# Merging stage, norm, router and the first context projections as ordered lists

## The reference, cut to what matters

```python
merged = merged + gates[:, :, n] * (o_n @ w_branch[l, n])          # four branches
x = layer_norm(DEEPNORM_ALPHA * x + merged @ w_out[l], ln1_g[l], ln1_b[l])
y = hierarchical_moe(x, r_group, r_group_b, r_expert, r_expert_b, e_gate, e_up, e_down)
x = layer_norm(DEEPNORM_ALPHA * x + y, ln2_g[l], ln2_b[l])
```

```python
h_c = modulate(rms_norm(x_ctx, g_attn[l]), csh1, csc1)      # 256 x 1024
p = h_c @ w_in                                              # c_q 768, c_kv 256, k_r 32, na 3 x 512, gates
mq = rms_norm(c_q, g_qa) @ w_uq ;  kv = rms_norm(c_kv, g_kva) @ w_ukv
# then attention over the context, its merge, its output product and its MLP
```

## Time and profile before

| | us |
|---|---|
| median of three runs | 4213.06 |
| the profiled execution's own time | 4211.14 |
| its span in the profile | 4209.2 |
| last product of the merge begins | 1024.00 |
| first product of the output stage begins | 1034.22 |
| first expert product begins | 1182.35 |
| sections 0 to 2 stand on TensorE | 1207.4 to 1251.4 |
| section 6's product | 1365.91 to 1379.9 |

### The profile page before, as it was taken

How to read it: one execution, slowest core, us unless ns; L and a number is a source line. 1 busy time by engine, 2 the same in 40 slices (tenths; PEclk the granted TensorE clock), 3 DMA queues, 4 the chain that set the end, 5 groups by cost and what they waited for, 6 DMA issues and landing times. The chain is left out here.

```text
span 4209.2 us, 38458 instructions
## 1 busy us (share of the span) xinstructions
PE 3767.7 (90%) x14796; PEld 2139.7 (51%) x14796; DVE 1752.0 (42%) x3047; ACT 757.3 (18%) x1690; POOL 169.3 (4%) x377
## 2 busy tenths in 40 slices
PE   7987777799578999999967899999998899999999
PEld 3653663444334344555533545458744455447844
DVE  0128643344413211111134655355446556445545
ACT  0212201111012211100113434110001354211000
POOL 1001000000010000000020300000000300000000
PEclk9989777799689999999988999999999999999999
DMA  7443001223157768888753111132222201122221
GB/s 297 174 159 112 1 5 50 95 95 130 72 203 295 282 240 326 350 343 344 305 201 109 61 41 40 70 110 80 80 80 86 103 21 61 58 83 80 80 80 60
DMA packets 197192, 574.67 MB, mean 137 GB/s; under 512 B 24324, under 2 KB 34356, under 8 KB 183752
## 3 DMA queue, kind: packets, MB, share of 16 engines
q1 hardware_dynamic: 177704, 518.35, 32.8%
q10 hardware_dynamic: 11424, 27.37, 1.9%
q0 software_dynamic: 7888, 26.53, 1.8%
HBM read 540.49 MB, written 31.73 MB: 136 GB/s over the span
## 5 line engine op out<-in xcount | busy, mean ns | idle before, releaser
L342 PE MATMUL ps<-out_sums 128*128 128x256 f32 (+1 forms) x1152 | 333.6, 450 | 2.3 <-issue 2.3
L342 PE MATMUL ps<-mixers_xT,ring 128*128 128x512 f32 (+2 forms) x928 | 306.9, 491 | 1.6 <-PEq L272 0.9
L342 PEld LDWEIGHTS ps<-out_sums 128*128 128x128 f32 x1152 | 218.7, 190 | 114.2 <-issue 94.5
L342 PEld LDWEIGHTS ps<-mixers_xT,ring 128*128 128x128 f32 (+1 forms) x928 | 173.5, 188 | 130.3 <-issue 115.2
L342 PE MATMUL ps<-ring,mixers_xT 128*128 128x512 f32 (+2 forms) x608 | 219.3, 517 | 9.9 <-DVE ab_qk L336 6.0
L342 PE MATMUL ps<-ring,layers_hT 128*128 128x512 f32 x416 | 186.7, 606 | 18.7 <-PEq L272 16.9
L2205 PE MATMUL ps<-ring,moe_xgT 128*64 128x512 f32 x432 | 191.8, 601 | 3.2 <-issue 2.3
L342 PEld LDWEIGHTS ps<-ring,mixers_xT 128*128 128x128 f32 x608 | 117.0, 205 | 108.6 <-issue 94.1
L342 PE MATMUL ps<-ring,out_hidden 128*128 128x512 f32 x384 | 167.4, 592 | 0.0
L2206 PE MATMUL ps<-ring,moe_xgT 128*64 128x512 f32 x368 | 163.1, 599 | 0.0
L342 PEld LDWEIGHTS ps<-ring,layers_hT 128*128 128x128 f32 x416 | 79.6, 194 | 120.0 <-issue 116.0
(11 more groups left out here) (895 smaller groups left out, 6170.1 us busy)
## 6 DMA issues: line engine op xcount, KB each, us to landing
ring<-in_w_ff SPq DMA_DIRECT2D x45, 2048.0 KB
ring<-in_w_in SPq DMA_DIRECT2D x40, 2048.0 KB
ring<-in_e_down SPq DMA_DIRECT2D x27, 2048.0 KB
ring<-in_e_gate SPq DMA_DIRECT2D x25, 2048.0 KB
ring<-in_e_up SPq DMA_DIRECT2D x25, 2048.0 KB
ring<-in_w_ada SPq DMA_DIRECT2D x24, 2048.0 KB
ring<-in_w_out SPq DMA_DIRECT2D x8, 2048.0 KB
deep_ring_more<-in_e_gate SPq DMA_DIRECT2D x8, 2048.0 KB, 7.8
```

What stands on the lines that cost most here:

```text
L342: last = pe.matmul(out, lhsT, rhs, start=(j == 0), stop=(j == len(pairs) - 1))
```

## The change

The merge's output stage becomes a single list. It begins with the transposes of half the merged rows, then the first four groups of the output product, the other transposes, the sums of rows. The norm is worked row tile by row tile inside the list; rows 0 and 1 are normed while the last products run. The seven products come in another order (the sixth pair, `out[5]`, ahead of `out[4]`). Between them stand the context's norm and its transposes (`work`, `turned`), and after them c_kv and k_r (`kv`, `kr`). The normed rows are stored by ScalarE, tile by tile.

The router becomes a list too, with the same steps, and c_q's four groups stand in it: one between the logits and the ranks, three behind the ranks. Section 6's product of near queries (`head`) stands ahead of the transposes of the first experts' rows. The weight tiles of sections 0, 1, 2 and 6 move forward accordingly. What is left of sections 0 and 2 (their norms) stays after pair 0's down product.

Some buffers move: the context's transposed rows have their own, its rows and the low-rank results lie in the branches' outputs, the experts' transposed rows in the first block's `xT`. The context rows are loaded twice: for the norm at the output stage's start, and again in the experts' block for the later residual, which waits for them (`x_landed`).

`CTX_COSTS` changes, and with it the places. Sections 3 to 5 now stand after pair 0, 6 (its norm) and 7 after pair 1, 8 after pair 2, 9 to 11 after pair 3, 12 to 14 after pair 4, none after pair 5, 15 and 16 after pair 6, 17 and 18 after 7, 19 and 20 after 8, 21 alone after 9, then two a pair after pairs 10 to 14, and 32 alone after pair 15.

```diff
+        flat = M.mixed[:, :, :, :].rearrange("p i k n -> p (i k n)")
+        self.low = flat[:, 0:TC * D].rearrange("p (t d) -> p t d", d=D)
+        self.x = flat[:, TC * D:].rearrange("p (t d) -> p t d", d=D)
+        self.q, self.ckv = self.low[:, :, 0:Q_LORA], self.low[:, :, Q_LORA:D]
+        self.hT = st.sb("c_hT", [P, DK, CTX])
+        self.k_r = st.sb("c_k_r", [P, TC, ROPE])
...
+        M.early = t0 + 2
 
         def load(sp):
-            sp.dma_start(x[:, :, :], by_rows(A["x"][0])).then_inc(st.sig["x"], 16)
+            for t in range(TC):
+                sp.dma_start(C.x[:, t, :], A["ctx_2"][0][t * P:(t + 1) * P, :]).then_inc(sig[f"c_x{t}"], 16)
+            sp.dma_start(x[:, :, :], by_rows(A["x"][0])).then_inc(sig["x"], 16)
...
-        made = row_sums(a, S)
-        gs, _, _ = seven(M, t0, t0 + 1, a, S, made, R, [parts[:, x_, 4, :] for x_ in range(2)],
-                         lambda x_, i, j: parts[:, x_, 2 * i + j, :], done)
-        products(M, "wout_p", made + sum(gs, []), tiles=2, extra={"sync": load})
-        layer_norm(M, "ln1", x, TT, A["ln1_g"][0], A["ln1_b"][0])
-        def save(sp):
-            sp.dma_start(by_rows(M.x1), x[:, :, :]).then_inc(st.sig["saved"], 16)
-            sp.wait_ge(st.sig["saved"], 16)
-        products(M, "x1T", transposes(M, lambda t, j: x[:, t, j * P:(j + 1) * P],
-                                      lambda j, a, n: M.xT[:, j, a * P:(a + n) * P], TT, DK),
-                 extra={"sync": save})
+        top, rest = (half_transposes(M, merged, M.xT, r) for r in range(2))
+        made = row_sums(a, S, tuple(top + rest))
+        out, ends, _ = seven(M, t0, t0 + 1, a, S, made, R, [parts[:, x_, 4, :] for x_ in range(2)],
+                             lambda x_, i, j: parts[:, x_, 2 * i + j, :], done)
+        for b in out[0]:
+            if b.pe:
+                b.needs += tuple(top)
+        def statistics(dve, link, t):
+            link.post(dve.bn_stats(stats[:, t, 0, :], x[:, t, 0:BANK]))
+            link(dve.bn_stats(stats[:, t, 1, :], x[:, t, BANK:D]))
+            return dve.bn_aggr(mv[:, t, :], stats[:, t, :, :])
+        def normalise(dve, link, t):
+            if t == 0:
+                dve.wait_ge(sig["gains"], 32)
+            link(dve.reciprocal(rs[:, t:t + 1], rs[:, t:t + 1]))
+            link(dve.tensor_scalar(x[:, t, :], x[:, t, :], mv[:, t, 0:1], rs[:, t:t + 1], ALU.subtract, ALU.mult))
+            link(dve.tensor_tensor(x[:, t, :], x[:, t, :], g[:, 0, :], ALU.mult))
+            return dve.tensor_tensor(x[:, t, :], x[:, t, :], g[:, 1, :], ALU.add)
+        counted = [group(None, lambda dve, _, link, t=t: statistics(dve, link, t), "v", after=(ends[t, 0], ends[t, 1]))
+                   for t in range(TT)]
+        roots = [group(None, lambda act, _, link, t=t: act.activation(
+            rs[:, t:t + 1], mv[:, t, 1:2], ACT.Sqrt, bias=M.ln_eps[:, :]), "s", after=(counted[t],)) for t in range(TT)]
+        normed = [group(None, lambda dve, _, link, t=t: normalise(dve, link, t), "v", after=(roots[t],))
+                  for t in range(TT)]
+        top1, rest1 = (half_transposes(M, x, M.xT, r, needs=tuple(normed[2 * r:2 * r + 2])) for r in range(2))
+        stores = [group(None, lambda act, _, link, t=t: act.dma_start(M.x1[t * P:(t + 1) * P, :], x[:, t, :]), "s",
+                        after=(normed[t],), dma=True) for t in range(TT)]
...
+        squares = Squares([C.low[:, t, :] for t in range(TC)])
+        work, scaled_ = rms_groups(M, st, "c_rms", C.x, TC, 1, D, load=lambda t: sig[f"c_x{t}"], share=squares)
+        turned = modulated(M, M.mod[0], TC, C.x, C.gain, 0, C.hT, s=1, needs=[(d, gained) for d in scaled_])
+        kv = row_groups(M, t0 + 2, 0, KV_LORA, C.hT, lambda t: C.ckv[:, t, :], on="s", rows=CTX, needs=turned)
+        kr = row_groups(M, t0 + 2, KV_LORA, ROPE, C.hT, lambda t: C.k_r[:, t, :], on="s", rows=CTX)
+        gs = top + out[0] + out[1] + rest + made + [gained] + work + out[2] + out[3] + out[5] + turned
+        gs += counted[0:2] + roots[0:2] + out[4][0:1] + normed[0:1] + out[4][1:] + normed[1:2] + out[6] + stores[0:2]
+        gs += kv[0:1] + top1 + counted[2:3] + roots[2:3] + kv[1:] + counted[3:] + roots[3:] + normed[2:] + kr
+        gs += stores[2:] + rest1
+        products(M, "wout_p", gs, tiles=3, extra={"sync": load})
...
+        chosen = group(logits, choose, "v")
+        weighed = group(None, exps, "s", after=(chosen,))
+        ranked = group(ranks, places, "v", needs=(chosen,))
+        gated = group(None, gates, "v", after=(weighed,))
+        t0 = M.weights.taken
+        cq = [row_groups(M, t0 + i, 0, n, C.hT, lambda t, c=c, n=n: C.q[:, t, c:c + n], on="s", rows=CTX)
+              for i, (c, n) in enumerate(((0, BANK), (BANK, 256)))]
+        products(M, "route_p", [chosen, weighed, cq[0][0], ranked, gated, cq[0][1], *cq[1]], tiles=2,
+                 extra={"sync": load, "gpsimd": tokens})
...
-        gs += turned[0]
+        gs += head + turned[0]
...
-CTX_COSTS = [10, 16, 8, 10, 13, 32, 16, 16, 40] + [0, 0, 32] * 2 + [16, 22] + [16] * 16
+EARLY = (0, 1, 2, 6)
+CTX_COSTS = [0, 0, 2, 10, 13, 32, 2, 16, 40] + [0, 0, 32] * 2 + [16, 22] + [16] * 16
...
-    order = []
+    order = [("ctx", i) for i in EARLY[3:]]
...
+    low_work, ups, keys, kT, v = latent_rows(0, tile(3))
+    sections.append([gained] + low_work)
+
+    q, cqT = C.q, cols_of(ins, 1536, Q_LORA // P)
+    cq_work, cq_made = rms_groups(M, st, "cq", q, TC, 1, Q_LORA, share=squares)
+    sections += [[], cq_work, ups]
...
+    head = qs if 6 in EARLY else []
+    sections += [([] if head else qs) + nq_work, ks + nk_work, vs + near + near_saves + mixed2]
...
+        tiles += [context[i] for i in EARLY[:3]]
```

More of the change, by code:

```diff
@@ new lines, in logits, with ranks @@
+        def logits(pe, bank):
+            pe.wait_ge(sig["w"], 32)
+            for t in range(TT):
+                last = matmuls(pe, bank[:, t * 36:(t + 1) * 36],
+                               [(M.xT[:, k, t * P:(t + 1) * P], w[:, k, :]) for k in range(DK)])
+            return last
+        def ranks(pe, bank):
+            pe.wait_ge(sig["iotas"], 1)
+            for t in range(TT):
+                matmuls(pe, bank[:, t * 32:(t + 1) * 32],
+                        [(M.ones[:, :], hot[:, 2, x, :]) for x in range(t)]
+                        + [(strict[:, :], hot[:, 2, t, :])])
+            return matmuls(pe, bank[:, 128:160], [(M.ones[:, :], hot[:, 2, x, :]) for x in range(TT)])
@@ L3603, in deep_order @@
     places = [2 * (pairs * sum(CTX_COSTS[:i]) // total) + 1 for i in range(len(CTX_COSTS))]
-    order = []
+    order = [("ctx", i) for i in EARLY[3:]]
     for n in range(pairs):
-        order += [("gate", n), ("up", n)] + [("ctx", i) for i, p in enumerate(places) if p == 2 * n]
-        order += [("down", n)] + [("ctx", i) for i, p in enumerate(places) if p == 2 * n + 1]
+        order += [("gate", n), ("up", n)]
+        order += [("down", n)] + [("ctx", i) for i, p in enumerate(places) if p == 2 * n + 1 and i not in EARLY]
     return order, places
@@ L3724, in attention, with landed @@
         return sum(attend(M, st, name, quads, 1, CTX, TC, (S, PT), ""), [])
-    sections = []
-    first, hT_made = normed("rms0", 0, 0, 0, wait=lambda t: sig[f"x{t}"])
-    low, low_work, ups, keys, kT, v = latent_rows(0, (tile(0), tile(3)), hT_made)
-    sections.append([gained] + first + low + low_work)
-    q, cqT = rows_of(ins, 0, Q_LORA), cols_of(ins, 1536, Q_LORA // P)
-    cq = [row_groups(M, tile(1 + i), 0, w, hT, lambda t, c=c, w=w: q[:, t, c:c + w], rows=CTX)
-          for i, (c, w) in enumerate(((0, BANK), (BANK, 256)))]
-    cq_work, cq_made = rms_groups(M, st, "cq", q, TC, 1, Q_LORA, made=list(zip(*cq)), share=squares)
-    sections += [cq[0], cq[1] + cq_work, ups]
+    def landed(dve, _, link):
+        for t in range(TC):
+            dve.wait_ge(sig[f"x{t}"], 16)
+        return dve.tensor_copy(gain[0:1, 0, 0, 1:2], gain[0:1, 0, 0, 1:2])
+    x_landed = group(None, landed, "v", after=(gained,))
+    sections = []
+    low_work, ups, keys, kT, v = latent_rows(0, tile(3))
[3 more added lines that the diff above has]
+    sections += [[], cq_work, ups]
     turned = transposes(M, lambda t, j: q[:, t, j * P:(j + 1) * P], None, TC, 6, needs=[(a,) for a in cq_made],
@@ L3781, in context_sections @@
         b.after += tuple(rows)
+    for b in outs[0]:
+        if b.tile == tile(15):
+            b.after += (x_landed,)
     after, hT_made = normed("rms1", 0, 1, 1, made=list(zip(*outs)))
-    sections += [rows + merged_T + outs[0], outs[1] + after]
+    sections += [rows + merged_T + [x_landed] + outs[0], outs[1] + after]
     hidden = [cols_of(ins, 2048 * i, DK) for i in range(2)]
```

273 lines of the change are left out of this document (132 added, 141 removed).

## The result

The changed kernel takes 4183.75 us (median of four runs, 4180.43 to 4185.21), against 4213.37 (4210.03 to 4215.85) for the kernel before beside it: a ratio of 0.9929, with an interval of 0.9912 to 0.9946. It is faster, by 0.7%, and 4183.75 lies inside the range of 4143 to 4186, but at its edge, and outside the forecast's own range of 4148 to 4173: 30 us were gained where 52 were forecast.

What follows compares the result with a forecast made beforehand. TensorE, busy 90% of the span, was taken as the bound, with idle waits at the first block's end. 6.4 + 1.3 + 35.0 + 13.9 - 5 = 51.6 us off 4211.1 gave 4159.5, said as 4160; range 4143 to 4186.

Steps and rivals of the forecast that it cites:

- The front: From the output stage's start to the first expert product, at 1175.9 instead of 1182.35: 6.4 us earlier.
- A: Rival: half clock all through the front, a price of 20 us, giving 4180; chance 0.15.
- C: Rival: starved pairs in the experts' stage, the bound of 25 us lost to tiles, giving 4180; chance 0.13.
- term for tiles: Experts' stage: pairs with few or no sections wait for weight tiles, 5 us lost; bounds 3 gained and 25 lost.
- the 20 of the sign: Sign of error: the prediction is wrong if waits for tiles sum to over 20 us.
- sections 0 to 2: Behind pair 0's down product: 44.0 us become norms alone, 9 left, 35 us gained; bounds 30 and 39.
- The fifth group: Output product: starts at about 1049.4 instead of 1048.2, behind copies of 0.7 and the first sum of rows, 1.23 us.
- my 0 to 4: Output stage: rows x come between 0 and 4 us later, behind 1 MB of context rows; 0 taken.
- the limit of 1106: Sign of error: the prediction is wrong if VectorE ends the norm later than 1106; 1102.1 was forecast.
- Rival B: Router's logits at full clock if work ahead keeps it up: 6.8 us, and 2.5 at c_q, giving 4151; chance 0.08.
- D: Rival: the ring paces the experts, 48.9 us come back as tile waits, front 12 us later, giving 4223; chance 0.04.
- pair 1's gate: Sign in the experts' stage: pair 1's gate comes about 43 us earlier than in the kernel before.

Runs made afterwards that it cites:

- hold_gate: The changed kernel with pair 0's second gate tile issued in the router's block, behind the router's own loads; 4184.27 us.
- hold_up: The changed kernel with pair 0's two up tiles issued in the experts' block, behind its small loads; 4180.55 us.
- lists_only: The changed kernel with all context work back in its old sections and costs, keeping lists, ScalarE stores and new product order; 4204.46 us.
- shift: The changed kernel with context sections placed by a written list: pair 5 has sections, pairs 7 and 8 one each; 4176.27 us.
- ones: The changed kernel with sections 15 to 18 placed one each after pairs 5 to 8, then two a pair; 4169.13 us.
- best: The placement of ones, with pair 0's second gate and two up tiles held back and the sums of rows two groups earlier; 4162.15 us.

## Why the prediction was right, and where it was short

The sum said 51.6 us; between the two profiled executions are 25.9, between the medians 30. Half of the mechanism held: the experts' stage stayed TensorE's, and it gave 34.1 us for the work taken out of it. The front did not: it was to give 6.4 us and cost 6.5 (5.6 of it behind the start of the list). It took in four sections' products and got longer, because a new wait, for small transfers beside weight tiles, came onto its path. The range held the result thanks to its width, which it had from the rivals A and C, both priced at 4180; neither of them is what happened. What is missing are 12.9 us in the front, 11.1 in the experts' stage and 1.7 behind it. The front, step by step from the same two lists of times:

| step | forecast | measured | short by |
|---|---|---|---|
| start of the list | 1029.4 | 1030.25 | 0.8 |
| from there to the norm's end | 72.7 | 75.2 | 2.5 |
| norm's end to logits | 8.9 | 13.1 | 4.2 |
| logits | 13.7 | 13.7 | 0 |
| first c_q group | 9.4 | 9.9 | 0.5 |
| ranks to slots | 9.5 | 9.6 | 0.1 |
| slots to the experts' block | 13.8 | 18.5 | 4.7 |
| near queries to first expert product | 18.5 | 18.6 | 0.1 |

**Tiles ahead of small transfers: 9 us, the step that failed.** The prediction took the block's end and the load behind it "as before", and the slots' way to the index at 13.8. Both are chains of small transfers for which a block waits at its end, and both had idle DMA engines before (a share of 0.00 to 0.02). I had looked at SyncE's queue, and wrote that its tiles are early enough for their reader. The question left out was what else moves while they do. The tile issued at 1102.47 meets the stores issued at 1102.5 and 1105.5, and the one at 1159.20 the scatters. The Trainium skill ("DMA: Bandwidth & Descriptors", section "Queues, rings and completion order") says that a DMA engine takes packets from its queues in turn. The runs show that transfers of several queues delay each other, not in what order the packets go: stores on ScalarE's queue took 10.4 us beside a tile and 4.2 without it. hold_gate, hold_up and lists_only each take the tile away from one or both places, and the wait goes with it.

**The experts' stage: 5 us of loss forecast, 16 measured.** The prediction named the places, and pairs 5 and 6 do wait, as case C had it. Its term for tiles came true in size: all waits for tiles in the stage, those under "issue" at an expert product included, sum to 17.5 us against 12.3 before, 5.2 more and under the 20 of the sign. Against the forecast of the stage, 11.1 us are missing. Idle time accounts for 4.4: the prediction gives 65.0 - 6.5 + 7 + 5 = 70.5, the window has 74.9, which is 65.0 - 6.5 + 6.3 (what is left of sections 0 to 2) + 5.2 (tiles) + 4.9 (ScalarE). Busy time accounts for the rest: 865.1 - 37.5 - 14.0 - 1.3 + 2 = 814.3 us were due, and it was 821.1; 0.9 of that are transposes left of sections 0 to 2, the rest is the clock. A wait of 4.7 us at 1563 costs more than itself, since the clock is low behind it (0.73 in the next 8.3 us, so 2.2 us more); I had priced waits for tiles without that. I had not priced the three waits of 1.63 us for ScalarE either, the 4.9 of above. They stand where section 21 is alone and shifts the order of the MLP sections behind it, and shift and ones, in which it is not, don't have them. The dip at 1390 is worth 5 us, and ones shows that it is not tied to the places. But the kernel before has one of its own (0.54 from 1461 to 1476, about 6 us) and none at 1390, so how much of the missing clock the change brought stays open.

**The fifth group: 1.9 forecast, 4.8 measured.** The copies and the first sum delayed it as the prediction says, by 2.98 us instead of 0.7 + 1.23, because VectorE took x late (2.79 us of wait, inside my 0 to 4) and the copies and adds queued behind it. The clock fell in the wait, which cost 1.8 more, and the prediction has nothing for that. best took out both. Of the 2.9 us that the forecast lacked here, 2.5 are left at the norm's end.

**What was right.** VectorE ended the norm at 1105.5, only just under the limit of 1106. The near queries took 16.7 us for 16.5. The ranks ran at full clock and took 3.1 us. Pair 0's gate and up took 13.9. Of sections 0 to 2 there remain waits of 4.01 and 2.27 us, 0.9 of transposes between them and some 2 of half clock in the next product (9.06 us, two groups of 3.5 at full speed), so 9 and not 44. Section 6's 14 us are gone. Rival B did not come: the logits took 13.87 us at 0.50. Its condition was not met, since the clock stood at 0.50 in the wait ahead of them (window 1109 to 1112), but TensorE was then busy in all 13 us of the window from 1119 and the clock did not come back. Rival A was wrong in all its terms: c_q's first group took 10.0 us where A has 13.9, and the ranks, the near queries and pair 0 were as forecast. D was wrong: the stage shrank by 34 of 49 us. C is the nearest rival, but its 20 us more of waits for tiles were not there. One sign was wrong in itself: pair 1's gate came at 1263.39, 12 us later than before and not 43 earlier, as the places that the change sets put sections 3 to 5 ahead of it.

## What to carry to other kernels

When work is moved ahead into idle time, its weight buffers come free there too, and the ring starts to fill them: look for the small stores, scatters and loads in that stretch that a block or a chain waits for, and hold the next large tile back behind them. Here that took 5 us off each of the two waits, which in the totals of four or five runs can't be told from their spread. When sections are taken out from between stages that live on prefetch, spread the rest one by one; a pair without filler waits, and TensorE's clock can fall in the wait. Price such a wait with the slow clock behind it: here 1.8 us more behind 2.98, and 2.2 more behind 4.69.

## What the runs showed of the hardware beyond that

- Two 512 KB stores landed after a median of 10.4 us while a 2 MB tile was on its way with the DMA engines at 0.93 to 1.01, and after 4.2 us without it. The wait behind the last of the eight scatters moved from 2.8 to 7.9 us in the same company, though they carry only row numbers.
- The clock fell to 0.50 in a stretch of some kernels and not of others with the same list: in 1390 to 1406 it was 0.63 in after and 1.00 in ones, with TensorE 14.23 and 13.79 us busy of 16. A dip of this size, 5 us, is as large as the effects of single edits here, and lies in one profile and not in another.
- The logits, 64 instructions of 36 columns, took 13.87 us at 0.50 in all nine changed kernels, directly behind a wait of 4 us as behind one of 9. In the kernel before they began at full clock (1.00 from 1119 to 1123, 0.61 from 1123 to 1126) and it fell to 0.50 although TensorE was busy: 13.66 us.
